# One kernel of a hybrid encoder: the end of the first mixer regrouped into quads of four heads

## The chip, the cores and the metric

The kernel runs on one core of a Trainium2 chip. Its time is that of one launch, in device microseconds, as the median of several runs. The core has a matrix engine (TensorE, PE in the profile; its weight loads are PEld), a vector engine (VectorE, DVE), a scalar engine (ScalarE, ACT) and a general engine (GpSimd, POOL). Transfers are issued by the sync queue (SP) and by some of the others. Every engine works through its own list of instructions in order, and waits on semaphores for the others.

## The reference

The input x has 256 tokens of 1024 numbers. Two layers follow, each a token mixer with a residual and then an expert layer (PEER) with a residual, and a last norm. The mixer of the first layer is a gated delta rule with 8 heads, run over the tokens forwards and backwards; what matters here is how it ends:

```
o = forward(q, k, v, g_f, beta_f) + backward(q, k, v, g_b, beta_b)   # 256 x 8 heads x 128
o = rmsnorm over the 128 numbers of each head (o) * norm_w * silu(z)
x = x + o.reshape(256, 1024) @ w_out
```

The mixer of the second layer is a state space scan (SSD). The expert layer takes top-16 keys of 8 heads and sums over 16384 experts; here both expert tables are streamed whole.

## The kernel before

Everything is float32 on 128 partitions. A token tile has 128 tokens, so there are two (t or c = 0, 1). Large products with weights from memory are made in split form: a weight block is cut by ACT into a high part (L1368) and by POOL or DVE into the rest (L1738, L900), and three matmuls stand for one. All weights come as one stream of 512 KB units in a ring of four slots, issued by SP; a unit is cut in two halves, and four halves are buffered in w_hi and w_lo.

The delta rule works on systems of 128 x 128, one for each direction d, head h and chunk c (32 in all). When the triangular systems are solved (the doubling loop with lines L1014 and L1029), the end of the mixer runs in steps. A quad is four heads of one direction, q4 = 2 * d + (h // 4), and has a PSUM bank:

1. U0: for each quad, solved system times v of the first chunk of the direction. DVE scales it by beta (L1058), POOL has scaled k (g_kS, L1776).
2. S1: k' times that gives the state after the first chunk; ACT copies it out of PSUM.
3. RQ: k and q of the second chunk times the state, into banks q4 and 4 + q4. DVE makes v - e^g * R (L1064, L1065) and hands it on; then, after all four quads, it scales the q part into g_inter (L1067).
4. U1: solved system times that; DVE scales by beta (L1071).
5. Output: for chunk c and half hg of the heads, two products for each head are summed in a PSUM bank, and DVE adds g_inter (L1078, b = 2 * c + hg).
6. Norm and gate: for each chunk t (8 heads), ACT squares each head's 128 numbers with a sum (L1528), DVE makes the mean (L1082), ACT the root (L1532), DVE a Newton step (polish, L852 to L856), the product with the reciprocal root (L1085) and with the gated z (L1089). g_siluz, silu(z) times the gain, has been made by ACT (L1520) and POOL (L1781).
7. PE transposes o (L604) into banks 0 to 3, ACT copies the high part into hT_hi (L1368), DVE the rest into hT_lo (L889).
8. out_row: 8 rows of the output weight, 12 matmuls of 512 columns each, into banks 4 to 7, then the residual (L908), the norm and the expert layer.

Before step 5, PE waits for all four quads at once. A chunk's steps 5 and 6 stand in DVE's list in this order, so that DVE adds for chunk 1 only when chunk 0 is gated. The two waits ahead of the output products are

```
pe.wait_ge(SEM["g_int"], 4)
pe.wait_ge(SEM["g_vn1"], 4)
```

Behind these steps, ACT's list has the splits of the weight stream (from the third unit of go on) and POOL's list has rest_of_units for them; SP loads a unit when an older one has been cut.

Of the kernel before, what the change touches and what calls it, by code (L numbers as in the profile page):

```python
# [33 lines left out]
P = 128  # L34
# [3 lines left out]
NT = T // P  # L38
# [65 lines left out]
def hybrid_encoder(nc, a, out):  # L104
    order, at, tables = weight_stream(a)
    ctx = ExitStack()
    with ctx:
# [107 lines left out]
        def by_block(v, level):  # L215
# [7 lines left out]
        g_o = g_TT[:, 0:16, :]  # L223
        g_sq = g_TT[:, 16:32, :]


# [77 lines left out]
            "g_tokps g_toksb g_sqsum g_mean g_root g_qk g_backps g_backsb g_bc g_minus g_E g_kq g_Ah g_A g_P g_mask g_Yps g_Y "  # L304
            "g_Zps g_TT g_eye g_XT g_Xps g_X g_kS g_U0 g_vn0 g_S1ps g_S1 g_RQ g_v1 g_int g_U1 g_vn1 g_Ops g_O g_osum g_omean g_oroot g_gz "
            "s_gate_ps s_gateb s_gexp s_yg s_zs s_centred s_conved s_silued s_gact s_da s_cum s_cumsb s_nac s_tokps s_toksb s_skip "
# [50 lines left out]
        def _(pe):  # L357
# [83 lines left out]
            def gdn():  # L441
# [116 lines left out]
                pe.wait_ge(SEM["g_TT"], LEVELS * GB)  # L558
                for q4 in range(4):
                    d, h0 = q4 // 2, 4 * (q4 % 2)  # L560
                    for e in range(4):
                        last = mm(PS[q4][:, e * P:(e + 1) * P], solved(d, h0 + e, d),
                                  g_tok[:, d, 2 * GH + h0 + e, :])
                    last.then_inc(SEM["g_U0"], 1)
                for q4 in range(4):
                    d, h0 = q4 // 2, 4 * (q4 % 2)
                    pe.wait_ge(SEM["g_vn0"], q4 + 1)
                    pe.wait_ge(SEM["g_kS"], q4 + 1)
# [4 lines left out]
                for q4 in range(4):  # L573
                    d, h0 = q4 // 2, 4 * (q4 % 2)
                    pe.wait_ge(SEM["g_S1"], q4 + 1)
# [6 lines left out]
                for q4 in range(4):  # L582
                    d, h0 = q4 // 2, 4 * (q4 % 2)
                    pe.wait_ge(SEM["g_v1"], q4 + 1)
                    for e in range(4):
                        last = mm(PS[q4][:, e * P:(e + 1) * P], solved(d, h0 + e, 1 - d),
                                  g_vp[:, d * GH + h0 + e, :])
                    last.then_inc(SEM["g_U1"], 1)
                pe.wait_ge(SEM["g_int"], 4)
                pe.wait_ge(SEM["g_vn1"], 4)  # L590
                pe.wait_ge(SEM["g_P"], GH)
                for c in range(NT):
                    for hg in range(2):
                        for e in range(4):
                            o = PS[4 + 2 * c + hg][:, e * P:(e + 1) * P]
                            f, r = system(0, 4 * hg + e, c), system(1, 4 * hg + e, c)
                            mm(o, g_tok[:, c, 4 * hg + e, :], g_vn[:, f, :], True, False)
                            last = mm(o, g_PTb[:, 4 * hg + e, c, :], g_vn[:, r, :], False, True)
                        last.then_inc(SEM["g_Ops"], 1)
                for t in range(NT):  # L600
                    pe.wait_ge(o_ready, t + 1)
                    for b in range(4):
                        for kk in range(2):
                            last = pe.transpose(PS[b][:, (2 * kk + t) * P:(2 * kk + t + 1) * P],  # L604
                                                g_o[:, t * GH + 2 * b + kk, :], ident)
                        if t == NT - 1:
                            last.then_inc(oT_psum, 1)
                pe.wait_ge(oT_lo, 4)
                for k in range(GH):
                    out_row("go", k, GH)  # L610

            def ssd():
# [104 lines left out]
                def turn_y(gi):  # L717
                    pe.wait_ge(o_ready, 2 + NT * (gi // 2 + 1))
                    if gi >= 4:
# [113 lines left out]
        def _(dve):  # L833
# [97 lines left out]
            def gdn():  # L931
# [123 lines left out]

                for q4 in range(4):
                    dve.wait_ge(SEM["g_U0"], q4 + 1)
                    dve.tensor_tensor(vn(q4, q4 // 2), bank(q4), quad(g_beta, q4, q4 // 2), ALU.mult).then_inc(SEM["g_vn0"], 1)  # L1058
                for q4 in range(4):
# [3 lines left out]
                    dve.wait_ge(SEM["g_RQ"], q4 + 1)  # L1063
                    link(dve.tensor_tensor(vp, bank(q4), quad(g_eg, q4, c), ALU.mult))  # L1064
                    dve.tensor_tensor(vp, g_tok[:, c, 2 * GH + h0:2 * GH + h0 + 4, :], vp, ALU.subtract).then_inc(SEM["g_v1"], 1)  # L1065
                for q4 in range(4):
                    dve.tensor_tensor(g_inter[:, 4 * q4:4 * q4 + 4, :], bank(4 + q4), quad(g_egq, q4, 1 - q4 // 2),  # L1067
                                      ALU.mult).then_inc(SEM["g_int"], 1)
                for q4 in range(4):
                    dve.wait_ge(SEM["g_U1"], q4 + 1)  # L1070
                    dve.tensor_tensor(vn(q4, 1 - q4 // 2), bank(q4), quad(g_beta, q4, 1 - q4 // 2), ALU.mult).then_inc(SEM["g_vn1"], 1)  # L1071
                dve.wait_ge(SEM["g_int"], 4)
                ss, ms, root, inv, new, rstd = (v[:, 0, :] for v in (g_ss, g_ms, g_root, g_inv, g_new, g_rstd))
                for t in range(NT):
                    for b in (2 * t, 2 * t + 1):
                        dve.wait_ge(SEM["g_Ops"], b + 1)
                        q = (1 - t) * GH + 4 * (b % 2)
                        dve.tensor_tensor(g_o[:, 4 * b:4 * b + 4, :], bank(4 + b), g_inter[:, q:q + 4, :], ALU.add).then_inc(SEM["g_O"], 1)  # L1078

                    s = slice(t * GH, (t + 1) * GH)  # L1080
                    dve.wait_ge(SEM["g_osum"], t + 1)
                    dve.tensor_scalar(ms[:, s], ss[:, s], 1.0 / P, EPS, ALU.mult, ALU.add).then_inc(SEM["g_omean"], 1)  # L1082
                    dve.wait_ge(SEM["g_oroot"], t + 1)
                    polish(ms[:, s], root[:, s], inv[:, s], new[:, s], rstd[:, s])
                    link(dve.tensor_tensor(g_o[:, s, :], g_o[:, s, :], wide(rstd[:, s], P), ALU.mult))  # L1085
                    if t == 0:
                        dve.wait_ge(SEM["g_gz"], 2)
                    v = flat(g_o[:, s, :], "s d")
                    dve.tensor_tensor(v, v, g_siluz[:, t, :], ALU.mult).then_inc(o_ready, 1)  # L1089
                for gi in range(4):  # L1090
# [275 lines left out]
        def _(act):  # L1366
# [59 lines left out]
            def gdn():  # L1426
# [92 lines left out]
                for t in range(NT):  # L1519
                    act.activation(g_siluz[:, t, :], g_siluz[:, t, :], ACT.Silu).then_inc(SEM["g_zs"], 1)  # L1520
                for q4 in range(4):
                    act.wait_ge(SEM["g_S1ps"], q4 + 1)
                    copy(g_S[:, 4 * q4:4 * q4 + 4, :], PS[4 + q4][:, :].rearrange("p (s d) -> p s d", s=4)).then_inc(SEM["g_S1"], 1)
                for t in range(NT):
                    for s in range(t * GH, (t + 1) * GH):
                        if s % 4 == 0:
                            act.wait_ge(SEM["g_O"], s // 4 + 1)
# [3 lines left out]
                    s = slice(t * GH, (t + 1) * GH)  # L1531
                    act.activation(g_root[:, 0, s], g_ms[:, 0, s], ACT.Sqrt).then_inc(SEM["g_oroot"], 1)  # L1532
                for b in range(4):
# [182 lines left out]
        def _(pool):  # L1716
# [56 lines left out]
            pool.wait_ge(SEM["g_U0"], 1)  # L1773
            for q4 in range(4):
# [108 lines left out]
```

## Time and profile before

| what | us |
|---|---|
| median of 3 runs | 2264.95 (2264.87 to 2265.81) |
| the profiled execution's own time | 2268.4 |
| its span | 2266.6 |
| PE busy | 2178.9 (96%) |
| DVE busy | 1476.7 (65%) |
| ACT busy | 1342.9 (59%) |
| POOL busy | 1069.7 (47%) |
| end of the first mixer: from the first U0 product to the first out_row product | 211.34 to 254.24 |

Times within the trace count from the span's start. In a row of the timeline the columns are the start, the time from start to end, engine, line, operation, what it writes and reads, the number of instructions merged, and in brackets the idle time before it with what released it. One float32 product of 128 x 128 is two records of the matrix engine. PEclk is the granted clock of TensorE: 1.00 is 2.4 GHz, 0.50 is 1.2 GHz.

### The profile page before, as it was taken

The numbers are of one execution on the slowest core, as the hardware profiler recorded it, in microseconds if no ns is written. First come the engines' busy times: TensorE is split into PE (matmuls) and PEld (weight loads), VectorE is DVE, ScalarE is ACT, GpSimd is POOL, SyncE is SP. The second block draws the span as 40 slices with busy tenths as digits, with TensorE's granted clock in tenths as the row PEclk, the third lists the DMA queues.
The fourth block names the chain that finished last, engine by engine and source line by source line (L and its number), as shares of the span: only waits on it lengthen the run. The fifth ranks groups of instructions, "written<-read, shape, count | busy, mean of one in ns | idle before, by whom it ended". The sixth has DMA issues, their size and how long they took to land.

```text
span 2266.6 us, 46015 instructions
## 1 busy us (share of the span) xinstructions
PE 2178.9 (96%) x14384; PEld 1984.3 (88%) x14384; DVE 1476.7 (65%) x3206; ACT 1342.9 (59%) x2734; POOL 1069.7 (47%) x827
## 2 busy tenths in 40 slices
PE   7989699999999999999899988999999999999998
PEld 6979599999999988888797767999999999888886
DVE  5756319985666577777765452199756665777776
ACT  6754355577777544444475664555687785444444
POOL 6841378987666600000065337799976665000000
PEclk9989899999999999999999999999999999999999
DMA  5510254555444566666544224555554445666664
GB/s 167 167 58 1 66 176 149 168 165 157 139 139 139 171 190 192 194 194 194 177 133 136 65 66 150 166 159 168 167 155 139 139 139 167 194 193 192 191 194 147
DMA packets 93872, 343.66 MB, mean 152 GB/s; under 512 B 10688, under 2 KB 10752, under 8 KB 93152
## 3 DMA queue, kind: packets, MB, share of 16 engines
q1 hardware_dynamic: 92592, 338.21, 48.5%
q0 software_dynamic: 912, 4.07, 0.6%
q8 instruction: 47, 0.77, 0.1%
q10 hardware_dynamic: 288, 0.34, 0.0%
q14 instruction: 33, 0.27, 0.0%
HBM read 341.53 MB, written 1.05 MB: 151 GB/s over the span
## 4 chain that ended last, share of the span: by engine, by line
PE 82%; POOL 7%; issue 5%; DVE 3%; ACT 2%; DMA 1%; POOLq 0%; DVEq 0%; ACTq 0%
PE bank L359 80%; POOL w_lo L1738 7%; PE bank L524 0%; PE bank L379 0%; DMA small<-in_ssd_d 0%; ACT w_hi L1368 0%; ACT arena L1394 0%; DVE arena L874 0%; ACT arena L1368 0%; DVE arena L989 0%; DVE arena L1190 0%; DVE arena L1029 0%; DVE arena L925 0%; DMA ring<-in_norm_final 0%; ACT arena L1528 0%
## 5 line engine op out<-in xcount | busy, mean ns | idle before, releaser
L1738 POOL TENSOR_TENSOR w_lo<-ring,w_hi 128x512 fp32r<-128x512 f32 x744 | 993.5, 1350 | 685.6 <-ACT w_hi L1368 673.9
L1368 ACT ACTIVATE w_hi<-ring 128x512 fp32r<-128x512 f32 x1280 | 804.4, 630 | 544.5 <-PE bank L359 542.7
L359 PE MATMUL bank<-hT_hi,w_hi 128*128 128x256 f32 x2688 | 780.0, 290 | 9.1 <-POOL w_lo L1738 7.0
L359 PE MATMUL bank<-hT_lo,w_hi 128*128 128x256 f32 x2688 | 761.3, 283 | 0.0
L359 PE MATMUL bank<-hT_hi,w_lo 128*128 128x256 f32 x2688 | 761.2, 283 | 0.0
L359 PEld LDWEIGHTS bank<-hT_hi,w_hi 128*128 128x128 f32 x2688 | 516.2, 192 | 20.1 <-POOL w_lo L1738 19.6
L900 DVE TENSOR_TENSOR w_lo<-ring,w_hi 128x512 fp32r<-128x512 f32 x536 | 374.9, 699 | 220.9 <-ACT w_hi L1368 213.9
L359 PEld LDWEIGHTS bank<-hT_lo,w_hi 128*128 128x128 f32 x2688 | 516.5, 192 | 0.0
L359 PEld LDWEIGHTS bank<-hT_hi,w_lo 128*128 128x128 f32 x2688 | 515.8, 192 | 0.0
L359 PE MATMUL bank<-w_hi,p_ag_hi 128*128 128x512 f32 x1024 | 398.4, 389 | 0.0
L359 PE MATMUL bank<-w_lo,p_ag_hi 128*128 128x512 f32 x1024 | 398.4, 389 | 0.0
L359 PE MATMUL bank<-w_hi,p_ag_lo 128*128 128x512 f32 x1024 | 398.3, 389 | 0.0
L359 PEld LDWEIGHTS bank<-w_hi,p_ag_lo 128*128 128x128 f32 x1024 | 192.2, 188 | 40.0
L359 PEld LDWEIGHTS bank<-w_lo,p_ag_hi 128*128 128x128 f32 x1024 | 192.2, 188 | 39.9
L359 PEld LDWEIGHTS bank<-w_hi,p_ag_hi 128*128 128x128 f32 x1024 | 192.2, 188 | 39.8
L1283 DVE TENSOR_TENSOR arena<-bank,arena 128x512 f32 (+1 forms) x128 | 88.6, 692 | 166.5 <-PE bank L359 166.5
L359 PE MATMUL bank<-arena 128*128 128x128 f32 (+2 forms) x1072 | 136.8, 282 | 8.0 <-ACT arena L1542 3.2
L359 PEld LDWEIGHTS bank<-arena 128*128 128x128 f32 x1072 | 133.3, 197 | 10.9 <-ACT arena L1542 3.4
L925 DVE SCALAR_TENSOR_TENSOR arena<-bank,small,arena 128x254 f32<-128x254 f32 x192 | 92.6, 482 | 50.7 <-ACT arena L1368 45.3
L1675 ACT ACTIVATE work<-work,small 128x128 f32<-128x128 f32 x256 | 113.3, 490 | 20.2 <-ACT work L1669 19.6
L1326 DVE TENSOR_TENSOR p_ag_lo<-arena,p_ag_hi 128x256 fp32r<-128x256 f32 x256 | 111.1, 434 | 8.9
L1648 ACT ACTIVATE work<-bank 128x256 f32<-128x256 f32 x144 | 55.5, 385 | 81.5 <-PE bank L359 81.5
(241 smaller groups left out, 2256.8 us busy)
## 6 DMA issues: line engine op xcount, KB each, us to landing
ring<-in_peer_u SPq DMA_DIRECT2D x256, 512.0 KB, 3.5
ring<-in_peer_v SPq DMA_DIRECT2D x256, 512.0 KB, 3.7
ring<-in_peer_wq SPq DMA_DIRECT2D x32, 512.0 KB, 3.5
ring<-in_gdn_qkv SPq DMA_DIRECT2D x24, 512.0 KB, 3.6
ring<-in_ssd_xbc SPq DMA_DIRECT2D x24, 512.0 KB, 3.6
ring<-in_ssd_z SPq DMA_DIRECT2D x16, 512.0 KB, 3.5
ring<-in_ssd_out SPq DMA_DIRECT2D x16, 512.0 KB, 3.6
ring<-in_gdn_z SPq DMA_DIRECT2D x8, 512.0 KB, 3.5
```

The lines of the kernel that those rows point to most:

```text
L359: return pe.matmul(o, w, r, start=first, stop=last)
L900: dve.tensor_tensor(w_part[1][:, s, :], ring[:, n % RING, hf * 512:(hf + 1) * 512], w_part[0][:, s, :].bitcast(F32), ALU.subtract).then_in ...
L925: ins = dve.scalar_tensor_tensor(o, bank[:, lo + s:hi + s], taps[:, m, j:j + 1], o, ALU.mult, ALU.add)
L1283: dve.tensor_tensor(v, PS[2 + q % 4][:, :].rearrange("p (t i) -> p i t", t=4), v, ALU.mult).then_inc(SEM["p_mul"], 1)
L1326: dve.tensor_tensor(p_ag[1][:, i % 2, :], v, p_ag[0][:, i % 2, :].bitcast(F32), ALU.subtract).then_inc(SEM["p_ag"], 1)
L1368: return act.activation(o, i, ACT.Copy, scale=scale)
L1648: act.activation(p_act[:, i % 2, :], PS[i % 2][:, 0:T], ACT.Gelu).then_inc(SEM["p_gelu"], 1)
L1675: act.activation(row, row, ACT.Relu, bias=p_T[:, 2, tok], scale=p_minus[:, tok]).then_inc(SEM["p_hotS"], 1)
L1738: pool.tensor_tensor(w_part[1][:, s, :], ring[:, n % RING, hf * 512:(hf + 1) * 512], w_part[0][:, s, :].bitcast(F32), ALU.subtract).then_i ...
```

## The change

Quads are taken in the order (2, 3, 0, 1), those of the backward direction first, in U0, S1, RQ, U1, in POOL's g_kS, ACT's copies and DVE's steps. The first output group (c = 0, hg = 0) needs the second chunk's result of quad 2, the second group that of quad 3, and so on; so PE waits before each output group for its own quad. The g_inter scaling goes from DVE (4 instructions of 128x512) to ACT (16 of 128x128, scale by column), in step with RQ. The output banks are those of the quads. A dummy Sqrt stands in ACT's list ahead of the squares. Of each chunk's two groups, ACT squares the first and DVE the second (a product and a tensor_reduce). There is one mean, one root and one Newton step for all 16 head sums, and the Newton step takes the reciprocal of the mean beside the root. The product with the gated z is made by POOL (4 of 128x512, into g_og), before the norm factor is known; DVE then multiplies by the factor in four instructions, in the order b = 0, 2, 1, 3. The transposes are made by half of the heads, four to a bank, after two of these; out_row waits for hT_lo by pairs of rows.

```diff
-                for q4 in range(4):
+                for i, q4 in enumerate(quads):
                     d, h0 = q4 // 2, 4 * (q4 % 2)
-                    pe.wait_ge(SEM["g_v1"], q4 + 1)
+                    pe.wait_ge(SEM["g_v1"], i + 1)
...
-                pe.wait_ge(SEM["g_int"], 4)
-                pe.wait_ge(SEM["g_vn1"], 4)
                 pe.wait_ge(SEM["g_P"], GH)
                 for c in range(NT):
                     for hg in range(2):
+                        pe.wait_ge(SEM["g_int"], 2 * c + hg + 1)
+                        pe.wait_ge(SEM["g_vn1"], 2 * c + hg + 1)
                         for e in range(4):
-                            o = PS[4 + 2 * c + hg][:, e * P:(e + 1) * P]
+                            o = PS[6 - 2 * c + hg][:, e * P:(e + 1) * P]
...
-                for t in range(NT):
-                    pe.wait_ge(o_ready, t + 1)
-                    for b in range(4):
+                for hg in range(2):
+                    pe.wait_ge(o_ready, 2 * (hg + 1))
+                    for b in (2 * hg, 2 * hg + 1):
                         for kk in range(2):
-                            last = pe.transpose(PS[b][:, (2 * kk + t) * P:(2 * kk + t + 1) * P],
-                                                g_o[:, t * GH + 2 * b + kk, :], ident)
-                        if t == NT - 1:
-                            last.then_inc(oT_psum, 1)
-                pe.wait_ge(oT_lo, 4)
+                            for t in range(NT):
+                                last = pe.transpose(PS[b][:, (2 * kk + t) * P:(2 * kk + t + 1) * P],
+                                                    g_og[:, t * GH + 2 * b + kk, :], ident)
+                        last.then_inc(oT_psum, 1)
                 for k in range(GH):
+                    if k % 2 == 0:
+                        pe.wait_ge(oT_lo, k // 2 + 1)
                     out_row("go", k, GH)
...
-                for q4 in range(4):
-                    dve.tensor_tensor(g_inter[:, 4 * q4:4 * q4 + 4, :], bank(4 + q4), quad(g_egq, q4, 1 - q4 // 2),
-                                      ALU.mult).then_inc(SEM["g_int"], 1)
...
+                def sum_squares(b):
+
+                    v = g_o[:, 4 * b:4 * b + 4, :]
+                    dve.wait_ge(SEM["g_O"], b + 1)
+                    link(dve.tensor_tensor(g_sq[:, 4 * b:4 * b + 4, :], v, v, ALU.mult))
+                    link(dve.tensor_reduce(ss[:, 4 * b:4 * b + 4], g_sq[:, 4 * b:4 * b + 4, :], AX.X, ALU.add))
+
+                for b in range(0, 4, 2):
+                    add_out(b)
+                    add_out(b + 1)
+                    sum_squares(b + 1)
+                dve.wait_ge(SEM["g_osum"], 2)
+                dve.tensor_scalar(ms, ss, 1.0 / P, EPS, ALU.mult, ALU.add).then_inc(SEM["g_omean"], 1)
+                dve.wait_ge(SEM["g_omean"], 1)
+                link(dve.reciprocal(inv, ms))
+                dve.wait_ge(SEM["g_oroot"], 1)
+                link(dve.tensor_tensor(inv, inv, root, ALU.mult))
+                link(dve.tensor_tensor(new, inv, root, ALU.mult))
+                link(dve.tensor_scalar(new, new, -0.5, 1.5, ALU.mult, ALU.add))
+                link(dve.tensor_tensor(rstd, new, inv, ALU.mult))
+                for b in (0, 2, 1, 3):
+                    dve.wait_ge(SEM["g_og"], b + 1)
+                    v = g_og[:, 4 * b:4 * b + 4, :]
+                    dve.tensor_tensor(v, v, wide(rstd[:, 4 * b:4 * b + 4], P), ALU.mult).then_inc(o_ready, 1)
...
+                for i, q4 in enumerate(quads):
+                    d, h0 = q4 // 2, 4 * (q4 % 2)
+                    act.wait_ge(SEM["g_RQ"], i + 1)
+                    for e in range(4):
+                        s = d * GH + h0 + e
+                        last = copy(g_inter[:, 4 * q4 + e, :], PS[4 + q4][:, e * P:(e + 1) * P], g_egq[:, 1 - d, s:s + 1])
+                    last.then_inc(SEM["g_int"], 1)
+                act.activation(n_idle, n_root, ACT.Sqrt)
+                for b in range(0, 4, 2):
+                    act.wait_ge(SEM["g_O"], b + 1)
+                    for s in range(4 * b, 4 * b + 4):
                         last = act.activation(g_sq[:, s, :], g_o[:, s, :], ACT.Square, accum_out=g_ss[:, 0, s:s + 1])
                     last.then_inc(SEM["g_osum"], 1)
-                    act.wait_ge(SEM["g_omean"], t + 1)
-                    s = slice(t * GH, (t + 1) * GH)
-                    act.activation(g_root[:, 0, s], g_ms[:, 0, s], ACT.Sqrt).then_inc(SEM["g_oroot"], 1)
+                act.wait_ge(SEM["g_omean"], 1)
+                act.activation(g_root[:, 0, :], g_ms[:, 0, :], ACT.Sqrt).then_inc(SEM["g_oroot"], 1)
...
+            pool.wait_ge(SEM["g_gz"], NT)
+            for b in range(4):
+                pool.wait_ge(SEM["g_O"], b + 1)
+                pool.tensor_tensor(flat(g_og[:, 4 * b:4 * b + 4, :], "s d"), flat(g_o[:, 4 * b:4 * b + 4, :], "s d"),
+                                   g_siluz[:, b // 2, (b % 2) * 512:(b % 2 + 1) * 512], ALU.mult).then_inc(SEM["g_og"], 1)
```

## Rows read from the trace of the kernel before

**Rows 1.** The page: the share of the chain that ended last, by engine.

```profile
PE 82%; POOL 7%; issue 5%; DVE 3%; ACT 2%; DMA 1%; POOLq 0%; DVEq 0%; ACTq 0%
```

**Rows 2.** That chain, 200 to 330 us: start us, us, what.

```profile
211.34 14.57 PE bank L359 x128
...
227.35 2.41 DVE arena L1067 x4
229.76 2.48 issue
...
243.82 2.46 ACT arena L1528 x16
...
254.24 22.74 PE bank L359 x90
```

**Rows 3.** The timeline of the matrix engine, 206 to 264 us.

```profile
211.34 18.13 PE L359 MATMUL bank<-arena 128*128 128x128 f32 x160 [0.78 <-DVE arena L1029]
232.24 7.38 PE L359 MATMUL bank<-arena 128*128 128x128 f32 x64 [2.77 <-issue]
243.24 1.09 PE L604 MATMUL bank<-const,arena 128*128 128x128 f32 x8 [3.62 <-DVE arena L1089]
250.34 1.97 PE L604 MATMUL bank<-const,arena 128*128 128x128 f32 x8 [6.01 <-DVE arena L1089]
```

**Rows 4.** The timeline of the vector engine, 206 to 264 us.

```profile
212.53 0.69 DVE L1058 TENSOR_TENSOR arena<-bank,small 128x512 f32<-128x512 f32 x1 [1.25 <-PE bank L359]
213.43 0.69 DVE L1058 TENSOR_TENSOR arena<-bank,small 128x512 f32<-128x512 f32 x1 [0.20 <-PE bank L359]
...
234.37 0.69 DVE L1078 TENSOR_TENSOR arena<-bank,arena 128x512 f32<-128x512 f32 x1 [2.23 <-PE bank L359]
236.09 0.69 DVE L1078 TENSOR_TENSOR arena<-bank,arena 128x512 f32<-128x512 f32 x1 [1.02 <-PE bank L359]
...
246.31 0.17 DVE L1082 TENSOR_SCALAR small<-small 128x8 f32<-128x8 f32 x1 [1.93 <-ACT arena L1528]
246.75 0.20 DVE L852 RECIPROCAL small<-small 128x8 f32<-128x8 f32 x1 [0.28 <-ACT small L1532]
246.99 0.17 DVE L853 TENSOR_TENSOR small<-small 128x8 f32<-128x8 f32 x1
...
249.06 1.23 DVE L1089 TENSOR_TENSOR arena<-arena 128x1024 f32<-128x1024 f32 x1
251.69 2.48 DVE L889 TENSOR_TENSOR hT_lo<-bank,hT_hi 128x512 fp32r<-128x512 f32 x4 [1.41 <-ACT hT_hi L1368]
```

**Rows 5.** The timeline of the scalar engine, 206 to 264 us.

```profile
235.10 0.31 ACT L1528 ACTIVATE arena<-arena 128x128 f32<-128x128 f32 x1 [15.71 <-DVE arena L1078]
...
238.11 1.28 ACT L1532 ACT_TABLE_LOAD   x1
...
251.06 2.07 ACT L1368 ACTIVATE hT_hi<-bank 128x512 fp32r<-128x512 f32 x4 [4.34 <-PE bank L604]
```

**Rows 6.** The timeline of GpSimd, 206 to 264 us.

```profile
216.64 4.67 POOL L1781 TENSOR_TENSOR arena<-arena,work 128x1024 f32<-128x1024 f32 x2
257.97 1.28 POOL L1738 TENSOR_TENSOR w_lo<-ring,w_hi 128x512 fp32r<-128x512 f32 x1 [36.65 <-ACT w_hi L1368]
```

**Rows 7.** The timeline of the scalar engine, 140 to 160 us.

```profile
141.22 1.15 ACT L1489 ACTIVATE arena<-bank,small 128x128 f32<-128x128 f32 x4 [0.22 <-PE bank L359]
```

**Rows 8.** Groups of the vector engine, 420 to 500 us: count, busy us, mean ns, idle before.

```profile
L1249 DVE TENSOR_TENSOR arena<-arena 128x512 f32<-128x512 f32 x16 | 27.2, 1766 | 0.1
...
L1250 DVE TENSOR_REDUCE arena<-arena 128x32 f32<-128x512 f32 x16 | 9.7, 677 | 0.1
```

**Rows 9.** The timeline of the vector engine, 1293 to 1296 us, while GpSimd works.

```profile
1293.99 1.38 DVE L900 TENSOR_TENSOR w_lo<-ring,w_hi 128x512 fp32r<-128x512 f32 x1 [0.89 <-ACT w_hi L1368]
```

**Rows 10.** Windows: PE, PEld, DVE, ACT, POOL busy, PEclk, DMA share, GB/s.

```profile
243.00:245.00 2.00, 1.09 (x8) 0.85 (x8) 1.38 (x3) 1.18 (x8) 0.00 (x0) 0.98 0.00 0
...
258.00:259.00 1.00, 1.00 (x5) 0.81 (x4) 0.00 (x0) 0.00 (x0) 1.00 (x1) 0.72 0.00 0
```

More of the change, by code:

```diff
@@ L224, in hybrid_encoder @@
         g_sq = g_TT[:, 16:32, :]
+        g_og = g_Y[:, 0:16, :]
+        quads = (2, 3, 0, 1)
         s_conv = tiny(SC, TAPS)
@@ L558, in gdn @@
                 pe.wait_ge(SEM["g_TT"], LEVELS * GB)
-                for q4 in range(4):
+                for q4 in quads:
                     d, h0 = q4 // 2, 4 * (q4 % 2)
@@ L564, in gdn @@
                     last.then_inc(SEM["g_U0"], 1)
-                for q4 in range(4):
+                for i, q4 in enumerate(quads):
                     d, h0 = q4 // 2, 4 * (q4 % 2)
-                    pe.wait_ge(SEM["g_vn0"], q4 + 1)
-                    pe.wait_ge(SEM["g_kS"], q4 + 1)
+                    pe.wait_ge(SEM["g_vn0"], i + 1)
+                    pe.wait_ge(SEM["g_kS"], i + 1)
                     for e in range(4):
@@ L572, in gdn @@
                     last.then_inc(SEM["g_S1ps"], 1)
-                for q4 in range(4):
+                for i, q4 in enumerate(quads):
                     d, h0 = q4 // 2, 4 * (q4 % 2)
-                    pe.wait_ge(SEM["g_S1"], q4 + 1)
+                    pe.wait_ge(SEM["g_S1"], i + 1)
                     c = 1 - d
@@ L581, in gdn @@
                     last.then_inc(SEM["g_RQ"], 1)
-                for q4 in range(4):
+                for i, q4 in enumerate(quads):
                     d, h0 = q4 // 2, 4 * (q4 % 2)
-                    pe.wait_ge(SEM["g_v1"], q4 + 1)
+                    pe.wait_ge(SEM["g_v1"], i + 1)
                     for e in range(4):
@@ L717, in turn_y @@
                 def turn_y(gi):
-                    pe.wait_ge(o_ready, 2 + NT * (gi // 2 + 1))
+                    pe.wait_ge(o_ready, 4 + NT * (gi // 2 + 1))
                     if gi >= 4:
@@ L1054, in vn @@
                     return g_vn[:, s:s + 7:2, :]
-                for q4 in range(4):
-                    dve.wait_ge(SEM["g_U0"], q4 + 1)
+                for i, q4 in enumerate(quads):
+                    dve.wait_ge(SEM["g_U0"], i + 1)
                     dve.tensor_tensor(vn(q4, q4 // 2), bank(q4), quad(g_beta, q4, q4 // 2), ALU.mult).then_inc(SEM["g_vn0"], 1)
-                for q4 in range(4):
+                for i, q4 in enumerate(quads):
                     d, h0 = q4 // 2, 4 * (q4 % 2)
@@ L1062, in gdn @@
                     vp = g_vp[:, 4 * q4:4 * q4 + 4, :]
-                    dve.wait_ge(SEM["g_RQ"], q4 + 1)
+                    dve.wait_ge(SEM["g_RQ"], i + 1)
                     link(dve.tensor_tensor(vp, bank(q4), quad(g_eg, q4, c), ALU.mult))
                     dve.tensor_tensor(vp, g_tok[:, c, 2 * GH + h0:2 * GH + h0 + 4, :], vp, ALU.subtract).then_inc(SEM["g_v1"], 1)
-                for q4 in range(4):
-                    dve.tensor_tensor(g_inter[:, 4 * q4:4 * q4 + 4, :], bank(4 + q4), quad(g_egq, q4, 1 - q4 // 2),
-                                      ALU.mult).then_inc(SEM["g_int"], 1)
@@ L1069, in gdn @@
-                for q4 in range(4):
-                    dve.wait_ge(SEM["g_U1"], q4 + 1)
-                    dve.tensor_tensor(vn(q4, 1 - q4 // 2), bank(q4), quad(g_beta, q4, 1 - q4 // 2), ALU.mult).then_inc(SEM["g_vn1"], 1)
[L1072 to L1078, printed above, removed]
-                    s = slice(t * GH, (t + 1) * GH)
[L1081 to L1089, printed above, removed]
@@ new lines, in gdn, with add_out @@
+                for i, q4 in enumerate(quads):
+                    dve.wait_ge(SEM["g_U1"], i + 1)
+                    dve.tensor_tensor(vn(q4, 1 - q4 // 2), bank(q4), quad(g_beta, q4, 1 - q4 // 2), ALU.mult).then_inc(SEM["g_vn1"], 1)
+                ss, ms, root, inv, new, rstd = (flat(v, "t c")[:, 0:2 * GH] for v in (g_ss, g_ms, g_root, g_inv, g_new, g_rstd))
+                def add_out(b):
+                    c, hg = divmod(b, 2)
+                    q4 = 2 * (1 - c) + hg
+                    dve.wait_ge(SEM["g_Ops"], b + 1)
+                    dve.tensor_tensor(g_o[:, 4 * b:4 * b + 4, :], bank(4 + q4), g_inter[:, 4 * q4:4 * q4 + 4, :], ALU.add).then_inc(SEM["g_O"], 1)
@@ L1773, in _ @@
             pool.wait_ge(SEM["g_U0"], 1)
-            for q4 in range(4):
+            for q4 in quads:
                 d, h0 = q4 // 2, 4 * (q4 % 2)
```

12 lines of the change are left out of this document (4 added, 8 removed).

## The prediction

> **What bounds the kernel now.** I read the page first. The chain that ended last is 82% matrix engine [rows 1], so for most of the 2266.6 us only fewer or faster matmuls would help. The change touches none of the large streams; it can pay only where the chain leaves the matrix engine. So I next read the chain in order of time around the first mixer's end [rows 2], and there it leaves it: from 227.35 us it runs over DVE (L1067), an issue gap of 2.48 us, a short piece of products, then squares, root, Newton step and gating, and comes back to the matrix engine only with the output rows at 254.24. Third, the timelines of the single engines [rows 3, 4, 5, 6] give the times at which each step starts, and the windows [rows 10] the granted clock. PE makes 80 products from 211.34 to 229.47, starts 32 output products at 232.24, makes 8 transposes at 243.24 and 8 at 250.34 [rows 3]. What sets the end in 229 to 254 is a serial walk between DVE, ACT and PE, done twice, once per chunk. Everything saved in this walk shifts the whole rest: the ring of weights is full and the cutters idle meanwhile (POOL had been idle for 36.65 us at 257.97 [rows 6]).
>
> **The change part by part.** I walk along the new schedule with the old durations. A DVE instruction that follows another through its own semaphore costs its duration and some 0.03 us.
>
> 1. Order of quads. Same work up to RQ; four products take 0.90 us (212.53 to 213.43 [rows 4]). 20 such groups from 211.34 end at 229.3. Nothing gained by itself: the order only makes the first output group depend on the quad that is done first.
>
> 2. g_inter from DVE to ACT. It takes 2.48 us (four of 0.62) out of DVE's list at 227.3, just between v - e^g R and the beta scaling [rows 2]. The cost on ACT: 16 scaled copies out of PSUM; the nearest row is an activation with the same shape and a scalar from SBUF, 4 in 1.15 us, 0.26 to 0.29 each in a row [rows 7], so 1.1 us a quad, while RQ delivers a quad each 1.8 us. ACT is idle there (for 15.71 us up to its first square at 235.10 [rows 5]), so this is hidden; the last is out some 1.3 us after RQ ends at 225.7. Without that cover it would cost 4.6 us. The dummy root then loads the table, 1.28 us [rows 5], at about 227 to 229, before the first add at 231.5. Hidden, and the load at 238.11 goes from the path.
>
> 3. The waits ahead of the output. DVE is free for the beta scaling at 227.35. The four quads of U1 come from 226.6 to 229.3, so the first two scalings are done by 228.8, before PE is through. The output starts at 229.34 instead of 232.24: **2.9 us**. Groups three and four need scalings that end by 230.3, and PE reaches them at 233. What is queued behind the waits is only the output itself.
>
> 4. Adds, squares, mean. From the start of the products to the first add are 2.13 us and to each next 1.72 us [rows 3, 4]. So adds become possible at 231.47, 233.19, 234.91 and 236.63. DVE: add to 233.91; the square product is a 128x512 instruction in SBUF, 0.69 + 0.03, to 234.63; the reduce is 0.68 + 0.02 [rows 8], to 235.33. So the third add starts 0.42 late and ends at 236.05; the fourth is on time and ends at 237.35. Squares to 238.07, reduce to 238.77. ACT's four squares of b = 2 end at 236.05 + 4 x 0.31 (2.46 for eight [rows 2]) = 237.3, inside that. The mean starts at **238.77** instead of 246.31. The first chunk's mean, root, Newton step and two long DVE products, some 7 us with its squares and its table load, are gone from the path.
>
> 5. From the mean to the last o_ready. Before: 246.31 to 250.29, 3.98 us [rows 4]. After: 0.44 to where the reciprocal stood (the reciprocal now lies beside the root), four links at 0.20 = 0.80 (three after the reciprocal's end [rows 4], one more for the new product), so 240.01; then four products at 0.63 (half of 1.23, and the gap). The first pair is ready at 241.27, the last at 242.53: 3.76 us. The width of 16 for 8 columns is bounded by 0 and 0.05 an instruction; I take 0.
>
> 6. Gate product on POOL. Nearest rows: 128x1024 in 2.33 us, thus 1.17 for 128x512, and a 128x512 subtract in 1.28 [rows 6]. They start with the adds' ends, 232.2, 233.9, 236.1, 237.4; the last ends at about 238.7 and is needed at 241.9 (b = 3 comes last). Hidden by mean, root and Newton step. If that cover went it would cost 1.3 us.
>
> 7. What POOL does to DVE. In 420 to 500 us, where POOL subtracts without pause, DVE's product of 128x512 with two inputs from SBUF takes 1.77 us in the mean (its inputs are broadcast, which may be part of it), and a plain subtract of 128x512 beside a working POOL took 1.38 [rows 9]; the same size takes 0.69 elsewhere, and the reduce, with one input, keeps 0.68 [rows 4, 8]. POOL's fourth gate product and DVE's fourth square product are released by the same add. Bounds: 0, when DVE goes first, and 1.08 to 1.3 when it waits behind POOL. DVE reacts to its own semaphore in 0.03 us, so I think it mostly goes first, with POOL then running into the small Newton products: I take **minus 0.4**. The second square product (b = 1) can be held too, but has slack up to the fourth add (0.6 us), so it adds at most 0.5. The Trainium skill ("SBUF — State Buffer", the section with the diagram of the ports) says that DVE with two SBUF inputs and GpSimd take a shared port pair as an exclusive lock, held for the whole instruction, and that the other fully blocks. By that rule alone the sum loses nothing or one whole gate product; the rows agree in direction, but neither 1.38 nor 1.77 tells a block from a slowdown.
>
> 8. Transposes and copies. Before, from o_ready at 250.29 to the first output row 3.95 us: 8 transposes at the low clock (1.97 us, twice 1.09 [rows 3]), with the copies of all four banks behind them (ACT 2.07, DVE 2.48, overlapping [rows 4, 5]). After: out_row needs only bank 0, which is transposed first, copied at about 242.5 to 243.1 and its rest made by 243.8. But PE's list has all 16 transposes ahead of out_row. At the low clock these are 16 x 0.246 = 3.94 us from 241.32: first row at **245.26**, against 254.24. The other three banks are needed 2.7 us or more later each: hidden.
>
> So the first output row comes 8.98 us earlier, 8.6 with the lock.
>
> 9. The clock. It fell at about 244.9 (0.98 in 243 to 245 [rows 10]), 5.3 us after the output products ended at 239.62, with 8 transposes between. It rose at about 258.6 (0.72 in 258 to 259 [rows 10]), 4.3 us after the output rows began. So 4.3 us of output rows ran at half speed: 2.1 us lost. After the change PE stands from 236.7 to 241.3, and I expect the fall in that time. Then the transposes run without a pause into the output rows, so by the same 4.3 us from 241.7 the rise is at 246.0, and if it takes the 5.3 that the fall took, at 247.0: only 0.3 to 1.3 us of output rows are slow, 0.15 to 0.65 lost. Of 1.5 to 1.95 I take **1.8 us** gained.
>
> 10. Behind. Splits and subtracts of the third unit on are released by half_used, so they move with PE; a subtract of 1.28 against 6 matmuls of about 0.23 = 1.37 leaves POOL 0.09 a half. The POOL gate products and ACT's copies are done before that. SP's ring is full either way. Effect 0.
>
> Sum: 8.6 + 1.8 = **10.4 us**. The profiled execution has 2268.4 for a span of 2266.6, 3.45 above the median of the runs; its time would become 2258.0, and the median 2264.95 - 10.4 = **2254.6**.
>
> **The rivals.**
> - *The clock holds.* After 3.6 us of idle (239.62 to 243.24) the first 8 transposes still ran at full clock [rows 3]; here the idle is 4.6. If it holds, only the second half of transposes counts, 242.53 + 0.4 + 0.05 + 1.09 = 244.1: 10.2 us, and all 2.1 of the clock: 12.3, so 2252.6. Against it: the idle is longer and ends with no products before it. 12%.
> - *The lock takes a whole gate product, and the clock rises late.* 8.98 - 1.3 = 7.7, and 0.8 of the clock, as when the rise comes 2 us later: 8.5, so 2256.5. For it: the rows of 420 to 500; against: POOL reads another engine's semaphore. 20%.
> - *The gain is given back further on.* The head start might be eaten where PE waits for POOL's subtracts (POOL has 7% of the chain [rows 1]). Then 0 to 4 us are left: about 2263. Against it: that work is released by the same norm, which moves along. 5%.
> - *Slower.* In the first route stage DVE's 128x512 products run against POOL's subtracts, 32 of the one kind and 1.77 for 0.69 [rows 8]: 34 us of a layer are such waiting. If the change makes the two fall worse on one another by x us for each, 32x is lost. From 15 us on, x = 0.47, it would outweigh the 10.4 and be slower by over 0.2%: 2269.5. Against it: both queues enter that stage from the same semaphores as before. 3%.
> - *It does not do what it says*, for instance the output products still start late because ACT's copies are slow: even at double price (9.2 us for 16) the first quad of g_inter is ready 2.3 us after 220.3. Within the last two.
>
> **How the numbers follow.** The forecast has 60%, the rivals 12, 20, 5 and 3. The forecast's own range is 2253.4 to 2255.8. The 8-in-10 range leaves out the last two cases and the ends of the others: 2252.3 to 2257.6. 0.2% is 4.5 us, about what a measurement of this kernel can tell from no change. Faster by more: 92%; within: 5%; slower: 3%.
>
> **What would show it.** In the new trace: output products start right behind U1, near 229.3, with no idle time before them (step 3); 16 ACT copies between 220 and 228 and a table load right behind (2); the mean, once and 16 wide, near 238.8 to 239.3 (4); the square product of b = 3 at 0.69, or at 1.4 or more if the lock bites (7); multiplications by the factor from 240 to 243 (5); transposes without a pause to the first output row near 245.5 (8); the clock up by 247 (9); from there on each event 10 us earlier than before (10). The prediction is wrong if the mean comes over 1 us later, if PE waits for POOL in the output rows, or if the 10 us seen at 270 us are not there at the end.

## The result and the profile after

The changed kernel takes 2254.56 us (median of 5 runs, 2252.69 to 2256.67) against 2265.81 us of the kernel before (5 runs, 2264.87 to 2270.93). The ratio is 0.9947, 95% interval 0.9933 to 0.9962: 12 us faster by the ratio, between 8.6 and 15.2; the two medians lie 11.2 apart. The forecast was 2254.6 and 10.4 us.

The matrix engine's timeline after, the rows that answer to [rows 3]:

```profile
208.40 25.28 PE L361 MATMUL bank<-arena 128*128 128x128 f32 x224 [0.78 <-DVE arena L1032]
...
238.82 3.68 PE L607 MATMUL bank<-const,arena 128*128 128x128 f32 x16 [5.14 <-DVE arena L1104]
...
242.15 0.78 PE L361 MATMUL bank<-w_hi,hT_hi 128*128 128x512 f32 x1
```

The products run from U0 to the end of the output in one piece; the gap of 2.77 us is gone. The transposes come once and go straight over into the output rows. The vector engine, which answers to [rows 4]:

```profile
228.35 0.69 DVE L1079 TENSOR_TENSOR arena<-bank,arena 128x512 f32<-128x512 f32 x1 [1.09 <-PE bank L361]
...
230.87 0.69 DVE L1085 TENSOR_TENSOR arena<-arena 128x512 f32<-128x512 f32 x1
...
232.31 0.69 DVE L1079 TENSOR_TENSOR arena<-bank,arena 128x512 f32<-128x512 f32 x1
...
234.44 0.69 DVE L1085 TENSOR_TENSOR arena<-arena 128x512 f32<-128x512 f32 x1
...
235.89 0.40 DVE L1093 TENSOR_SCALAR small<-small 128x16 f32<-128x16 f32 x1
...
237.47 2.49 DVE L1104 TENSOR_TENSOR arena<-arena,small 128x512 f32<-128x512 f32 x4
```

ACT and GpSimd beside it, from the same timeline:

```profile
223.00 1.14 ACT L1383 ACTIVATE arena<-bank,small 128x128 f32<-128x128 f32 x4 [0.65 <-PE bank L361]
224.15 1.28 ACT L1546 ACT_TABLE_LOAD   x1
...
229.19 1.27 POOL L1806 TENSOR_TENSOR arena<-arena 128x512 f32<-128x512 f32 x1 [10.82 <-DVE arena L1079]
230.91 1.78 POOL L1806 TENSOR_TENSOR arena<-arena 128x512 f32<-128x512 f32 x1 [0.45 <-DVE arena L1079]
233.08 3.17 POOL L1806 TENSOR_TENSOR arena<-arena 128x512 f32<-128x512 f32 x2 [0.39 <-DVE arena L1079]
```

ACT's four scaled copies keep up with RQ (1.14 us a quad, then idle for 0.65), and the table load behind them ends 3.6 us before the first square, which starts at 229.08. GpSimd's gate product takes 1.27 us where DVE doesn't square beside it and 1.78 where it does. The last one ends at 233.08 + 3.17 = 236.25, and DVE's mean, which took 0.17 before [rows 4], ends at 236.29.

To compare kernels I use times counted from the first U0 product of each profile (us; "rest" is from the first residual add, L908 before, to the end of the span; "withheld" is read from the windows of the rest, 10 us wide: what the granted clock lacks of 1.00, times the width, added up):

| kernel | first add | mean | transposes | first output row | residual add | rest | withheld |
|---|---|---|---|---|---|---|---|
| before | 23.03 | 34.97 | 39.00 | 42.90 | 65.66 | 1989.6 | 27.7 |
| changed | 19.94 | 27.48 | 30.41 | 33.74 | 55.76 | 1988.7 | 27.7 |
| changed, again (c_after) | 19.95 | 27.48 | 30.41 | 33.61 | 54.33 | 1987.4 | 24.4 |
| e1, front undone | 22.96 | 30.49 | 33.42 | 36.66 | 57.51 | 1984.3 | 22.8 |
| e2, norm undone | 19.95 | 31.94 | 35.97 | 39.85 | 62.20 | 1988.8 | 27.7 |
| e3, gate on DVE | 19.95 | 27.48 | 31.64 | 35.92 | 58.42 | 1988.9 | 27.5 |
| e4, squares on ACT | 19.96 | 27.35 | 30.06 | 33.39 | 54.14 | 1983.9 | 20.9 |
| e5, order 0 to 3 | 20.17 | 27.70 | 30.64 | 33.96 | 55.78 | 1981.7 | 17.5 |
| e6, no dummy root | 19.95 | 27.48 | 30.42 | 33.75 | 54.46 | 1984.1 | 20.9 |
| e7, wait for all | 19.95 | 27.48 | 30.41 | 35.50 | 58.25 | 1989.4 | 27.8 |
| e8, one gap filled | 19.95 | 27.49 | 30.43 | 32.50 | 53.23 | 1981.5 | 17.5 |
| e10, all gaps filled | 19.95 | 27.35 | 30.06 | 32.13 | 52.85 | 1979.7 | 6.9 |
| e11, 1 us of delay in the rest | 19.96 | 27.49 | 30.43 | 33.62 | 54.33 | 1990.5 | 27.8 |
| e12, 2 us of delay in the rest | 19.95 | 27.49 | 30.42 | 33.75 | 55.67 | 1991.8 | 29.2 |

(Mean and transposes are the second ones where there are two. Times agree with the rows to 0.01.) Up to the first output row the control repeats the first profile within 0.13 us; behind it, it doesn't. So the first four columns show what an edit does. The residual add has a spread of its own of 1.4 us: in five profiles of the same code up to there, or the same but for the dummy root (changed, c_after, e6, e11, e12), the output rows take 22.02, 20.72, 20.71, 20.71 and 21.92 us. The rest column says nothing of an edit; it follows the column beside it.

### The profile page after: what moved, and what is told of

Same layout as the page of the kernel before. It is cut to its first block, busy times and chain, and to the rows that moved or that the text cites. A ratio compares the mean times of both kernels' runs of the same rounds, so it can differ in the third digit from the quotient of the medians.

```text
span 2252.9 us, 46022 instructions
## 1 busy us (share of the span) xinstructions
PE 2175.5 (97%) x14384; PEld 1982.0 (88%) x14384; DVE 1474.7 (65%) x3200; ACT 1341.0 (60%) x2734; POOL 1076.0 (48%) x831
## 4 chain that ended last, share of the span: by engine, by line
PE 83%; POOL 7%; issue 5%; DVE 2%; ACT 2%; DMA 1%; POOLq 0%; DVEq 0%; ACTq 0%
PE bank L361 81%; POOL w_lo L1759 7%; PE bank L526 0%; PE bank L381 0%; ACT w_hi L1383 0%; DMA small<-in_ssd_d 0%; DVE arena L877 0%; ACT arena L1383 0%; DVE arena L992 0%; DVE arena L1205 0%; ACT arena L1409 0%; DVE arena L1032 0%; DVE arena L928 0%; DMA ring<-in_norm_final 0%; PE bank L450 0%
```

## The experiments

**e1, the front undone.**

```diff
+                pe.wait_ge(SEM["g_int"], 4)
+                pe.wait_ge(SEM["g_vn1"], 4)
                 pe.wait_ge(SEM["g_P"], GH)
...
-                        pe.wait_ge(SEM["g_int"], 2 * c + hg + 1)
-                        pe.wait_ge(SEM["g_vn1"], 2 * c + hg + 1)
...
+                for q4 in quads:
+                    dve.tensor_tensor(g_inter[:, 4 * q4:4 * q4 + 4, :], bank(4 + q4), quad(g_egq, q4, 1 - q4 // 2),
+                                      ALU.mult).then_inc(SEM["g_int"], 1)
...
```

ACT's 16 scaled copies go; DVE does this work again.

> The changed kernel with its front part undone: g_inter is scaled by DVE again and the matrix engine waits for all four quads before the first output product; the norm, gate and transposes stay as changed. Theory A (the front part is worth what its place on the path says): the output products start 2.9 us later after the first U0 product than in the changed kernel, and everything behind follows; from the first U0 product to the first output row 36.6 us against 33.7 in the changed kernel and 42.9 before; time about 2257.5 us, 8 below the kernel before. Rival B (the head start is swallowed by the serial norm, so that only the norm part pays): 33.7 us, time as the changed kernel.

Measured: first output row at 36.66, 2.9 us later than changed and just as theory A had it. The median is 2253.99 (2252.67 to 2254.23), ratio 0.9946 (0.9933 to 0.9960): no later than the changed kernel. The 2257.5 of theory A was wrong, though rival B's 33.7 was wrong too. The stretch shows where it was lost: the output rows took 20.85 us (57.51 - 36.66) against 22.02, and the rest 1984.3 against 1988.7. Its timeline has the old gap back:

```profile
229.96 7.38 PE L361 MATMUL bank<-arena 128*128 128x128 f32 x64 [2.77 <-issue]
```

**e2, only the front** (squares, root, gate and transposes by chunk, as before).

> The changed kernel with only its front part: quads in the new order, g_inter on ACT, waits by quad; squares, root, gate and transposes by chunk as before. Theory A: from the first U0 product to the first output row 40.0 us (42.9 less 2.9), and the time 2.5 to 3.5 us below the kernel before. Rival B (the front part pays nothing alone): 42.9 us and no difference.

Measured: 39.85, 3.05 less than before; 2262.74 us (11 runs), ratio 0.9986 (0.9977 to 0.9995), 3.2 us faster. Theory A in both numbers. The two parts add up: e2, the front alone, brings the first row 3.05 us forward and e1, all but the front, 6.24, together 9.29; the changed kernel has 9.16.

**e4, all squares on ACT.**

```diff
...
-                for b in range(0, 4, 2):
-                    add_out(b)
-                    add_out(b + 1)
-                    sum_squares(b + 1)
-                dve.wait_ge(SEM["g_osum"], 2)
+                for b in range(4):
+                    add_out(b)
+                dve.wait_ge(SEM["g_osum"], 4)
...
-                for b in range(0, 4, 2):
+                for b in range(4):
                     act.wait_ge(SEM["g_O"], b + 1)
```

> The changed kernel, but ACT squares all four groups and DVE none. Theory A (the split of the squares pays nothing): ACT needs 1.28 us for the last group where DVE needs 1.42, the third add is no longer late, and the mean no longer runs into GpSimd's last gate product (0.40 instead of 0.17 us); the stretch from the first U0 product to the first output row is 33.3 us against 33.7. Rival B (two engines are needed, because ACT falls behind with four groups): 34.9 us or more.

Measured: first row at 33.39, theory A: the second engine for the squares buys nothing and costs 0.35 us. The mean takes 0.17 again, with GpSimd's last product just done, and without DVE's squares GpSimd's four products take 1.26 to 1.27 us each:

```profile
237.98 0.17 DVE L1084 TENSOR_SCALAR small<-small 128x16 f32<-128x16 f32 x1 [1.34 <-ACT arena L1541]
```

The median is 2251.05 us (2250.63 to 2251.49), ratio 0.9934 (0.9920 to 0.9948).

**e3, the gate product on DVE.**

```diff
...
-                    dve.wait_ge(SEM["g_og"], b + 1)
                     v = g_og[:, 4 * b:4 * b + 4, :]
-                    dve.tensor_tensor(v, v, wide(rstd[:, 4 * b:4 * b + 4], P), ALU.mult).then_inc(o_ready, 1)
+                    link(dve.tensor_tensor(v, g_o[:, 4 * b:4 * b + 4, :], wide(rstd[:, 4 * b:4 * b + 4], P), ALU.mult))
+                    f = flat(v, "s d")
+                    dve.tensor_tensor(f, f, g_siluz[:, b // 2, (b % 2) * 512:(b % 2 + 1) * 512], ALU.mult).then_inc(o_ready, 1)
...
```

GpSimd's four products go.

> The changed kernel with the gate product back on DVE: after the root, DVE multiplies each group by the factor and then by the gated z (8 instructions of 128x512 instead of 4), GpSimd does none. Theory A: the mean costs 0.17 instead of 0.40 us because GpSimd is idle, the last pair is ready 2.6 us later, and the first output row comes 1.7 us later: 35.4 us behind the first U0 product against 33.7. Rival B (DVE's product and GpSimd's are equal, since GpSimd blocks DVE's ports): 33.7.

Measured: 35.92, 2.2 us later (1.7 expected: the second half of the transposes now waits for its pair until 34.30). The mean takes 0.17 us with GpSimd idle:

```profile
236.32 0.17 DVE L1093 TENSOR_SCALAR small<-small 128x16 f32<-128x16 f32 x1
```

So the 0.40 of the changed kernel is GpSimd's doing: 0.23 us. The median is 2258.03 (2254.61 to 2259.95), ratio 0.9962 (0.9948 to 0.9976).

**e5, the order of quads**: `quads = (0, 1, 2, 3)`, and the first chunk's output groups wait for 3 and 4 of g_int and g_vn1.

> The changed kernel with the quads in the old order 0, 1, 2, 3, and the output groups of the first chunk waiting for the third and fourth quad (g_int and g_vn1 of 3 and 4) instead of the first and second. Theory A (the order is worth next to nothing, because the third beta scaling ends 0.1 us after U1): the first add comes at 20.1 us behind the first U0 product against 19.95, the first row at 33.9. Rival B (the order is what frees the output): 1 us later, the time of one more scaling.

Measured: 20.17 and 33.96: the order is worth 0.22 us, near theory A, far from B. One run, 2247.99 us, which is lower than the changed kernel's with a later first row.

**e6, no dummy root**: the line `act.activation(n_idle, n_root, ACT.Sqrt)` ahead of the squares goes.

> The changed kernel without the dummy root ahead of the squares. In the kernel before, the table load stands right behind the squares, before the mean is there. Theory A (the load doesn't wait for the mean, and hides behind DVE's squares): first row 33.7 us behind the first U0 product, nothing lost. Rival B (the load falls on the path): 0.5 to 1.3 us later.

Measured: 33.75, theory A. One run, 2250.88 us. The load stands behind the last square and is over before the mean is there:

```profile
236.37 1.28 ACT L1552 ACT_TABLE_LOAD   x1
238.36 0.22 ACT L1552 ACTIVATE small<-small 128x16 f32<-128x16 f32 x1 [0.70 <-DVE small L1093]
```

It hides behind DVE's square and reduce; with all squares on ACT it would have only DVE's mean to hide behind. That pairing wasn't run.

**e7, one wait for hT_lo.**

```diff
+                pe.wait_ge(oT_lo, 4)
                 for k in range(GH):
-                    if k % 2 == 0:
-                        pe.wait_ge(oT_lo, k // 2 + 1)
```

> The changed kernel, but the matrix engine waits for all four parts of hT_lo before the first output row, as the kernel before does. Theory A: the fourth part is ready at 35.5 us behind the first U0 product (243.85 in the changed kernel), so the first row starts at 35.5 against 33.7, 1.8 us later, and the matrix engine stands for 1.4 us at the low clock. Rival B (the copies overlap the transposes as before, nothing changes): 33.7.

Measured: 35.50, theory A, and 2258.39 us (2257.17 to 2258.62), ratio 0.9961 (0.9947 to 0.9975).

**e8, the gap ahead of the transposes filled.**

```diff
+                for _ in range(22):
+                    mm(PS[0][:, 0:P], ident, ident)
                 for hg in range(2):
                     pe.wait_ge(o_ready, 2 * (hg + 1))
```

> The changed kernel with 22 products of the identity with itself (128x128, into bank 0, nobody reads them) on the matrix engine between the last output product and the transposes, 4.9 us of the 5.1 in which it stood idle. Theory A (the low clock behind the idle time still costs the changed kernel 2.4 us): the clock stays at 2.4 GHz, the transposes take 1 us less on the path and the output rows lose no 1.4 us; first output row 32.7 us after the first U0 product, and the residual add 2.4 us earlier than in the changed kernel; time about 2252. Rival B (the clock falls all the same, or the fillers delay the transposes): 33.7 us or more and no gain.

Measured: first row at 32.50, residual add at 53.23, 2.5 us before the changed kernel: theory A. Against the control (c_after, below) it is 1.1 us in both columns, because there the clock is back before the first output row. So the filled gap is worth 1.1 to 2.5 us here. The time is 2248.28 us (2247.16 to 2252.81), ratio 0.9927 (0.9914 to 0.9941), lower than the 2252 that the stretch accounts for; the rest is 7.2 us shorter, with 17.5 us withheld for 27.7. Windows of the changed kernel, then of e8 (columns as in [rows 10]):

```profile
238.00:240.00 2.00, 1.18 (x6) 1.18 (x7) 1.97 (x4) 0.03 (x1) 0.00 (x0) 0.52 0.00 0
...
242.00:244.00 2.00, 2.00 (x7) 1.62 (x6) 1.53 (x3) 0.87 (x2) 0.00 (x0) 0.50 0.00 0
244.00:246.00 2.00, 2.00 (x8) 1.63 (x7) 0.00 (x0) 0.63 (x1) 0.14 (x1) 0.77 0.00 0
```

```profile
240.00:242.00 2.00, 1.75 (x16) 1.45 (x14) 2.00 (x4) 0.28 (x1) 0.00 (x0) 1.00 0.00 0
242.00:244.00 2.00, 1.89 (x14) 1.64 (x13) 1.82 (x4) 1.88 (x4) 0.00 (x0) 1.00 0.00 0
```

With the gap filled the clock stays at 2.4 GHz over transposes and output rows.

**c_after, the changed kernel again.**

> The changed kernel again, unaltered, as a control for what differs between two profiled executions of the same code. Expected by all: the stretch from the first U0 product to the first residual add 55.8 us within 0.5, as in its first profile; the median within 2 us of 2254.56. Open, and read here: how far the start of that stretch (208.4 us in the first profile, 211.3 before) and the rest behind it (1988.7 us) move by themselves.

Measured: 2252.58 us (2248.57 to 2254.29), ratio 0.9938 (0.9926 to 0.9951). The residual add is at 54.33, 1.4 us earlier than in the first profile and outside the 0.5 expected, and the first U0 product stands at 210.71 instead of 208.41. Its windows:

```profile
240.00:242.00 2.00, 0.88 (x4) 0.88 (x5) 2.00 (x4) 0.00 (x0) 0.00 (x0) 0.69 0.00 0
242.00:244.00 2.00, 2.00 (x12) 2.00 (x11) 1.20 (x3) 1.21 (x3) 0.00 (x0) 0.50 0.00 0
244.00:246.00 2.00, 2.00 (x11) 1.72 (x10) 1.76 (x3) 1.18 (x2) 0.00 (x0) 0.95 0.00 0
```

0.95 in 244 to 246 puts the rise at 244.2, 3.1 us behind the first transpose (241.12); in the first profile 0.77 puts it at 244.9, 6.1 us behind (238.82). The same code, the same gap, and 2.8 us or none of the output rows at 1.2 GHz.

**e11 and e12, a plain delay** of 5 or 10 linked DVE instructions in the norm behind the mixer:

```diff
                 dve.wait_ge(n_sq, 2 * NT * (i + 1))
+                if i == 1:
+                    for _ in range(5):
+                        link(dve.tensor_scalar(n_new, n_inv, 1.0, None, ALU.mult))
```

> The changed kernel with 5 small linked DVE instructions (a tensor_scalar of two columns, nobody reads the result) in the norm behind the first mixer: a plain delay of 1.0 us on the path. Theory A (what the rest takes depends on where the clock's falls land on it, and a shift moves them): the stretch from the residual add to the end is not simply 1.0 us longer but may come out several us shorter or longer, with falls of the granted clock inside the second mixer (1260 to 1300 us) that come or go. Rival B (the rest follows the code alone): 1.0 us longer than in the control, within 0.5.

> As the 1 us delay, with 10 instructions: 2.0 us. Theory A: again not the sum, and another value than for 1 us; theory B: 2.0 us longer than the control, within 0.5.

Measured: the rest is 1990.5 and 1991.8 us, against 1988.7 and 1987.4 for the unaltered code, so 1.8 to 3.1 and 3.1 to 4.4 longer, for delays of 1.0 and 2.0. The medians are 2257.09 (2255.06 to 2257.67) and 2257.48 (2248.21 to 2259.43). Rival B fails: both are outside its 0.5, against either profile of the unaltered code. More than the sum, as A allows, and the withheld clock of the rest has risen too, from 24.4 in the control to 27.8 and 29.2. But A had named falls of the clock at 1260 to 1300 us that come and go, and there they don't: 1200 to 1300 us has a clock of 0.93 in both, in the control and in the first profile. The control differs from them behind 1300 us (0.95 for 0.93 in 1300 to 1440).

**e10, all gaps filled and squares on ACT**: 21 to 25 such products in each of six gaps, ahead of the solve loop, of the transposes of both mixers and of the transposes behind three norms.

> A version meant to beat both: squares on ACT alone, and products of the identity that nobody reads in each of the 5.5 to 6 us in which the matrix engine stands idle (ahead of the solve loop, the transposes of the first mixer, the transposes of the second mixer, and the three norms). Theory A (each such idle time costs the low clock in what follows, 1 to 2 us each): the low clock is nearly gone behind 150 us and the time falls by 1 to 2 us for each of the five further places below the 2248.3 us with one place filled: 2240 us. Rival B (the clock falls anyway, or fillers are late): 2248 or more.

Measured: 2241.67 us (4 runs, 2240.43 to 2243.56), ratio 0.9895 (0.9881 to 0.9909): 23.8 us below the kernel before and the best of the study. By the medians it gives 6.6 us over e8, which has one gap filled and squares on both engines, at the low end of the 5 to 10 expected for five further gaps; counted from the kernel before in each one's own round it is 5.6. Of the profiled spans, 4.6 us apart, 2.5 lie ahead of the first U0 product, 0.4 in the stretch and 1.8 in the rest. The mean granted clock of its executions is 0.996 to 0.999, against 0.984 to 0.985 for the changed kernel.

## Why the prediction was right

The mechanism was right, and most terms were; one term was right only as a size that the same code has sometimes. That the median came within 0.1 us of the forecast is luck: the changed kernel's five executions spread over 4 us and the control has 2252.58, and the median hides differences that cancel. The first row came 0.6 us earlier than forecast, the clock's term was 1.1 smaller in the profile, and 3.8 us lie outside the stretch, where I had nothing.

- *Steps 1 and 2* held. RQ, U1 and ACT's copies run as costed; the order of quads is worth 0.22 us (e5), where I had nothing.
- *Step 3* (2.9 us): the first add comes at 19.94 instead of 23.03, 3.1 us. e2, which has this part alone, gains 3.05 in the stretch and 3.2 us in time.
- *Step 4*: the mean was put 27.43 us behind the first U0 product and measured at 27.48. The third add was late by 0.4 as foreseen; e4 shows that ACT alone does as well, which the prediction's own numbers would have said, had I walked it: four squares of 0.31 behind the fourth add's end at 237.35 end at 238.6, DVE's square and reduce at 238.77.
- *Step 5*: 2.55 us from mean to transposes, measured 2.93. Of the difference, 0.23 is the mean's; the other 0.15 is spread over the root, the four links and the first two products.
- *Steps 6 and 7*: GpSimd's gate product is hidden; on DVE it costs 2.2 us (e3). Of the lock's 0.4 us, 0.23 came, at another place: DVE's square product went first and kept its 0.69, GpSimd's was stretched from 1.27 to 1.78, and DVE's mean, whose turn came behind it, ended as GpSimd's last product did. e4 has no squares on DVE, and there GpSimd's products keep 1.27 and the mean 0.17. The direction agrees with what the Trainium skill ("SBUF — State Buffer", the section with the diagram of the ports) says of an exclusive lock; the size nearly does. Blocked for the whole of DVE's square, GpSimd's second product would end at 231.56 + 1.27 = 232.83; it ended at 232.69. But the mean has one input tensor, so if it is the lock, it is that of the 2-port modes of DVE that the section also names. No run here tells that apart from another cause in GpSimd's traffic.
- *Step 8*: 3.94 us for the 16 transposes, measured 3.33 to the first output row; I had taken the time of 8 with the tail of the last. With this the first row came at 33.74, where 33.92 without the lock and 34.3 with it were forecast: 9.2 us earlier against 8.6. The wait by pairs, on which the step rests, is worth 1.8 us (e7).
- *Step 9*, the clock's 1.8 us, is the term that was mis-sized in the first profile. The output rows took 22.02 us instead of 22.76 before: 0.74. The rise came 6.1 us behind the first transpose, not 4.3 to 5.3. In the control it came 3.1 us behind, the rows took 20.72 and the term was 2.0. The kernel before has one profile here, so its 22.76 has an unknown spread of its own. The clock did fall in the gap in both, so the rival in which it holds did not happen; e8 shows what it would have given, 1.1 to 1.2 us to the first row and 1.1 to 2.5 to the residual add, where I had 1.9.
- *Step 10*: the stretch ends 9.9 us earlier (11.3 in the control) and the whole 12 us. The rest of the difference of the profiled spans (13.7) is 2.9 us ahead of the first U0 product, in code that wasn't changed, and 0.9 behind. Ahead of it the granted clock differs as well: 0.93 in 100 to 205 us before and in the control, 0.97 in the changed kernel's first profile, whose U0 product comes earliest of the three. The U0 product stands between 208.1 and 211.3 in these profiles, and the rest between 1987.4 and 1988.7 for the same kernel, down to 1984.1 for e6, whose stretch is the same within 0.15 us up to the first row.

The rest and the medians move by 3 to 7 us between kernels that differ by tenths up to the first output row (e5 and e6 against changed). The profiles show where: in the clock. Over all kernels but e10, the withheld clock of the rest goes from 17.5 to 29.2 us, and the rest goes with it from 1981.5 to 1991.8, somewhat less than one for one. In windows of 50 us the clock is 1.00 from 300 to 1100 us and from 1450 to 2200 in every profile; these kernels differ ahead of 300 and in 1200 to 1450. The changed kernel, then e8, where the work is the same (columns as in [rows 10]):

```profile
1200.00:1300.00 100.00, 96.82 (x430) 69.35 (x429) 46.58 (x70) 60.20 (x140) 37.52 (x38) 0.93 0.27 84
```

```profile
1200.00:1300.00 100.00, 96.20 (x452) 68.16 (x451) 49.11 (x75) 63.50 (x149) 38.27 (x39) 1.00 0.27 85
```

One and the same kernel does this too: of the six executions of e12 five took 2255.19 to 2259.43 us at a mean clock of 0.983 to 0.984, and one 2248.21 at 0.988. What sets the moment at which the clock falls and rises stays open. So the medians of e1 against the changed kernel say nothing about the front part; its columns do.

## What to carry to other kernels

In this serial walk between engines, regrouping paid what the rows said to within 0.6 us in 9: split a wait so that the first consumer waits for the first producer, make one statistic instead of two, and put what doesn't need it (the gate) on an idle engine. Then check each part alone: here the second engine for the squares, the dummy root and the order were worth -0.35, 0 and 0.22 us, and the waits by quad, the single norm, the gate on GpSimd and the wait by pairs carried it. Where the matrix engine idled for 5 us in this walk, products that nobody reads, ended before the next real one, were worth 1.1 to 2.5 us at one place. And an edit of a few microseconds is read in its own stretch: the whole time of one and the same kernel moved by more, with the clock.

## What the runs showed that I had not expected

- The clock's rise behind the same gap came 3.1 us after the work resumed in one profile of the changed kernel and 6.1 us in another, 1.3 us of output rows apart (20.72 and 22.02).
- A one-input DVE instruction of 128x16 took 0.40 us beside a working GpSimd and 0.17 without it, while GpSimd's 128x512 product took 1.78 us beside DVE's 128x512 square and 1.27 alone.
- Filling six idle gaps of the matrix engine with 144 products that nobody reads made the kernel faster, not slower: 2241.67 us against 2251.05 for e4, which has the same real work, at a mean granted clock of 0.996 to 0.999 against 0.985 to 0.987.
- Six executions of one kernel (e12) lay 11 us apart, and their mean granted clock went with the time: 0.983 for the longest, 0.988 for the shortest.
